# Moving where the tiles start in SBUF in a two-layer transformer kernel

## The chip, the cores and the metric

The kernel runs on one core of one Trainium2 chip. The metric is the device time of one execution in microseconds (us); lower is better. Engines are named as in the profile: PE is the matrix engine (its weight loads are shown apart as PEld), DVE the vector engine, ACT the scalar engine, POOL the general-purpose engine, and SP the engine that issues most of the DMAs. SBUF is the on-chip memory of 128 partitions. A tile takes the same bytes in each of its partitions, so its place is one number: the byte at which it starts in a partition.

## The reference

Two transformer layers are applied to one sequence of 512 positions and 1024 features, with 256 further positions of memory. The first layer is

```python
x = x + 0.5 * swiglu_ffn(rmsnorm(x, ffn1_norm_g), ffn1_w_in, ffn1_w_out)
h = rmsnorm(x, mix_norm_g)                      # q, kv, gates, conv, q_mem, merge gates = h @ w_in
x = x + (g_nsa * o_nsa + g_conv * o_conv + g_mem * o_mem) @ w_out
x = x + 0.5 * swiglu_ffn(rmsnorm(x, ffn2_norm_g), ffn2_w_in, ffn2_w_out)
```

where `o_nsa` is causal attention of 16 heads in three parts (compressed, selected and windowed keys), `o_conv` a gated convolution of width 3, and `o_mem` attention to the memory. The second layer is

```python
x = x + _mixer_block(_rms(x, norm_mix_w), ...)  # windowed attention with sinks + gated linear attention
x = x + _memory_xattn(_rms(x, norm_mem_q_w), _rms(mem, norm_mem_kv_w), ...)
x = x + _swiglu(_rms(x, norm_ffn_w), w_ffn_gate, w_ffn_up, w_ffn_down)
return _rms(x, norm_final_w)
```

All of it is given and returned in float32.

## The kernel before

**Arithmetic.** Activations are kept transposed, with features on partitions and the 512 positions along the row. Each matrix product is made of three matmuls of operands that are split in two: `three` sends high times high, high times low and low times high into one PSUM bank. So each 128x128 piece of weight costs three weight loads and three matmuls of 512 columns.

**Weights.** A unit is one DMA of up to 128x1024 floats from HBM into one of four tiles `raw`. ACT copies it into one of three tiles `whi`, rounded (`split` of `act_program`, line 1372), and DVE writes the remainder into `wlo`, which has the same place as `raw` (`split` of `dve_program`, line 1734). `dense` then makes 24 matmuls of it: for each k from 0 to 7 the stationary operand is the slice of 512 bytes at 512k of the unit, and the moving operand is a row of 2048 bytes of the activations, `XH[:, k, :]` or `XL[:, k, :]`.

**Order of the work.** The function `order` writes one list of work items, and each engine's program runs through this list. Five programs are issued, tied by semaphores. Nothing in them looks at the place of a tile.

**Places.** `sb` allocates a tile behind the last one. `place` sets a tile at a fixed column of one large block, the arena, whose first byte is `base`; the stages of the kernel use the arena in turn. In it are `RX` (the products of the two halves of each FFN, read by 1584 matmuls of the three FFNs), `MG`, `OA`, `OG` and `OM` (the operands of the output projections), `PM`, `PS`, `PW`, `P2` and `PCT` (attention weights), keys, queries, values, the tiles `pp` and `pw` of the softmax, the bias tables `TB`, the memory (`FX`, `ME`), the convolution's `CB`, and at its end the four tiles `raw`/`wlo`. Behind it stand `whi`, `XT`, `XH`, `XL`, `RB`, `cst` (constants, the identity among them), five temporary tiles `tmp`, and small tiles.

Ahead of the arena stand `vec` (176 columns of gains, biases and taps, used as per-partition scalars), `relx`, `negs` and `bg2`. A statement checks that `base` is a multiple of 1024.

**Small tiles.** `sn` is four scratch tiles for the inverse square roots; `rsqrt` uses their rows 0 to 4 (line 1762), and `rsq_out` (line 2410) gives the row of the result, row 5 of 6.

Of the kernel before, what the change touches and what calls it, by code (L numbers as in the profile page):

```python
# [14 lines left out]
P = 128  # L15
# [5 lines left out]
KF = HF // P  # L21
BIG = 1e30
EPS = 1e-6
ARENA = 28928
C_ID, C_INV, C_SEL, C_C1024, C_C256, C_ANY, C_END = 0, 128, 256, 258, 259, 260, 261


# [50 lines left out]
NVEC = _n  # L78
# [636 lines left out]
def build(nc, A, out):  # L715
# [4 lines left out]
    def sb(name, shape, dt=F32):  # L720
        return stack.enter_context(nc.sbuf_tensor("t_" + name, shape, dt))[:]

    vec = sb("vec", [P, NVEC])
    relx = sb("relx", [33, 16])
    negs = sb("negs", [P, 16])
    bg2 = sb("bg2", [P, 16])
    base = (nc.sbuf_base + 31) // 32 * 32
    assert base % 1024 == 0
    sb("arena", [P, ARENA + NRAW * UNIT])

    def place(name, at, cols, dt=F32):

        assert at + cols <= ARENA + NRAW * UNIT
        return nc.alloc_sbuf_tensor_at("t_" + name, [P, cols], dt, offset=base + 4 * at)[:]
# [3 lines left out]

    raw = [place(f"raw{i}", ARENA + i * UNIT, UNIT) for i in range(NRAW)]
    wlo = [place(f"wlo{i}", ARENA + i * UNIT, UNIT, F32R) for i in range(NRAW)]  # L740
    whi = [sb(f"whi{i}", [P, UNIT], F32R) for i in range(NHI)]
# [2 lines left out]
    XL = sb("XL", [P, KD, S], F32R)  # L744
    RB = sb("RB", [P, S])
    cst = sb("cst", [P, C_END])
    T = [sb(f"tmp{i}", [P, S]) for i in range(5)]
    FX = place("FX", 0, 5632)
    RX = place("RX", 6656, 22016, F32R)
# [25 lines left out]
    CB = [place(f"CB{q}", 19328 + q * S, S) for q in range(2)]  # L775
    CBS = [T[2:4]] * EARLY + [CB] * (KD - EARLY)
    QS = [place(f"QS{q}", (26624, 20480)[q], 2048, F32R).rearrange("p (h n) -> p h n", h=4) for q in range(2)]
# [14 lines left out]
    PW = place("PW", 12800, 4096, F32R)  # L792
    KFT = [place(f"KF{q}", 16896 + 512 * q, 512) for q in range(2)] + [T[4]]
    VW = place("VW", 17920, 2560, F32R)
# [11 lines left out]
    P2 = place("P2", 8704, 4096, F32R)  # L806
    OM = [place(f"OM{q}", 12800 + q * 1024, 1024, F32R).rearrange("p (k n) -> p k n", k=2) for q in range(2)]
    sa = [sb(f"sa{i}", [P, 8]) for i in range(RING)]
    sn = [sb(f"sn{i}", [P, 6, 16]) for i in range(4)]
    rn = sb("rn", [P, 9 * 8])  # L810
    gn = sb("gn", [P, 4, 48])
    gqn = sb("gqn", [P, 6])
    vcn = sb("vcn", [P, 64])
    vch = sb("vch", [P, 64], F32R)
    csm = sb("csm", [P, 4, 4, 4])
    KC = [sb(f"kc{q}", [P, P], F32R) for q in range(2)]
    banks = Banks([stack.enter_context(nc.psum_tensor(f"bank{i}", [P, 512], F32))[:] for i in range(8)])
    xs = nc.dram_tensor("x_kept", [D, S], F32, kind="Internal").ap()
# [75 lines left out]
    def squares(what, h, q):  # L894
        if what == "k":
            return T[h][:, 256 * q:256 * q + 256]
        return T[q] if h else T[2 + q]

# [8 lines left out]
    def pe_program(e):  # L907
# [3 lines left out]
        def mm(o, l, r, start, stop):  # L911
            return e.matmul(o, l, r, start=start, stop=stop, skip_group_check=True)  # L912
# [61 lines left out]
        def stat(item, parts, nt, g, sel, role="s"):  # L974
            b = take(role, item)
            n = len(parts) * g
            o = b[:, 0:nt * n].rearrange("p (i h) -> p i h", i=nt)
            for q, ap in enumerate(parts):
                for i in range(nt):
                    f = mm(o[:, i, q * g:(q + 1) * g], ap[:, i * P:(i + 1) * P], sel, True, True)  # L980
            f.then_inc(*full.tick(item))

        def nstat(ni):
            on.wait_ge(*calc.at(("nacc", ni, 7)))
            on.wait_ge(*d_c.at(0))
            stat(("nstat", ni), [T[4]], 4, 1, cst[:, C_C1024:C_C1024 + 1])

# [40 lines left out]
        def widefin(what, h):  # L1028
            on.wait_ge(*calc.at(("rs", "w", what, h)))
            nt = 2 if what == "k" else 4  # L1030
            spread(("widefin", what, h), rsq_out(("w", what, h), nt, 1), nt, 0, 1)
# [150 lines left out]
        def gnt():  # L1182
            b = take("d", ("gn",))
            on.wait_ge(*curve.at(("ng",)))
            for i in range(4):
                f = e.transpose(b[:, i * P:(i + 1) * P], T[4][:, i * P:(i + 1) * P], ident)
            f.then_inc(*full.tick(("gn",)))
# [8 lines left out]
        def sqfin(g, q):  # L1196
            on.wait_ge(*calc.at(("rs", "sq", g)))
            spread(("sqfin", g, q), rsq_out(("sq", g), 4, 4), 4, 2 * q, 2 * q + 2)
# [8 lines left out]
        def skfin(half, a):  # L1207
            on.wait_ge(*calc.at(("rs", "sk", half)))
            spread(("skfin", half, a), rsq_out(("sk", half), 4, 4), 4, 2 * a, 2 * a + 2)
# [4 lines left out]
        def cscore(g):  # L1214
# [3 lines left out]
            for i in range(4):  # L1218
                n = 8 * i + 8
                for r in range(4):  # L1220
                    o = b[:, i * P + r * 32:i * P + r * 32 + n]
                    l = QS[g % 2][:, r, i * P:(i + 1) * P]
                    mm(o, l, KC[0][:, g * 32:g * 32 + n], True, False)
                    f = mm(o, l, KC[1][:, g * 32:g * 32 + n], False, True)
            f.then_inc(*full.tick(("cscore", g)))
# [142 lines left out]
    def act_program(e):  # L1368
        on = Once(e)

        def copy(o, i, **how):
            return e.activation(o, i, ACT.Copy, **how)  # L1372
# [146 lines left out]
        def kc2():  # L1519
            on.wait_ge(*calc.at(("kc", 4)))  # L1520
            copy(KC[0], KX).then_inc(*x_hi.tick(("kc",)))

# [204 lines left out]
    def dve_program(e):  # L1727
# [9 lines left out]
        def low(o, x, hi, item, *more):  # L1737
            on.wait_ge(*x_hi.at(item))
            e.tensor_tensor(o, x, f32(hi), ALU.subtract).then_inc(*x_lo.tick(item, *more))  # L1739
# [267 lines left out]
        def kc2():  # L2007
# [7 lines left out]
            on.wait_ge(*calc.at(("kc", 4)))  # L2015
            low(KC[1], KX, KC[0], ("kc",))

# [384 lines left out]
    slot = {}  # L2402
# [4 lines left out]
            slot[key] = len(slot) % 4  # L2407

    def rsq_out(R, nt, n):
        return sn[slot[R]][:, 5, 0:nt * n].rearrange("p (i h) -> p i h", i=nt)  # L2410

    signals = [full, w_hi, w_lo, x_hi, x_lo, evac, copied, curve, calc, scaled, zeroed, cleared, *d_raw, *d_x, *d_m, *d_s, *d_b, *d_o,
               d_c, d_vec, d_rel, d_oh, d_w2, d_g, *d_tb, d_mask, d_gc, d_lrw]
# [91 lines left out]
```

## Time and profile before

| | us |
|---|---|
| median of three executions | 2558.79 |
| lowest, highest | 2556.7, 2560.76 |
| profiled execution | 2556.7 |
| its span, first to last instruction | 2554.9 |

The profiled execution is the fastest of the three; 1.8 us of it lie outside its span. Busy time says for how long an engine had an instruction at work; the chain of waits says which work the end waited for. Matmuls overlap each other in the profile: one of 512 columns is shown with some 390 ns though the next starts some 227 ns later. So the distance from start to start, in the timeline, is what a matmul costs in a full stretch, and its shown duration also counts the time in which it lies behind the one before it.

### The profile page before, as it was taken

To read this page: it belongs to the slowest core of one execution; us is meant where nothing else is said; L and a number is where in the kernel's file an instruction comes from. 1 tells how busy PE (TensorE), PEld (TensorE's weight loads), DVE (VectorE), ACT (ScalarE), POOL (GpSimd) and SP (SyncE) were. 2 spreads that over 40 slices of the span, in tenths; PEclk is the share of its full clock that TensorE was granted. 3 is DMA by queue.
4 is the path that set the end of the run, shared out by engine and by line. 5 is a ranking of instruction groups with operands and counts; after the bars stand their busy time and mean duration, and the time that the engine had idled before them with its cause. 6 is when DMAs were issued, how large, how long until landed. Compare 5 with 4: busy or idle time off the path is not lost.

```text
span 2554.9 us, 31373 instructions
## 1 busy us (share of the span) xinstructions
PE 2460.6 (96%) x12046; PEld 2055.1 (80%) x12046; DVE 1412.0 (55%) x2965; ACT 962.9 (38%) x1784; POOL 173.1 (7%) x236
## 2 busy tenths in 40 slices
PE   7999999999999999989999999999998997999997
PEld 6888888888887878778888888878876886788886
DVE  5435555676567566765443446666543566543444
ACT  4323334432344444553322334655422345322321
POOL 0000000100001111220000000222100002000000
PEclk9999999999999999999999999999998999899998
DMA  3454433333321111103223224211121341223222
GB/s 131 119 123 128 111 110 137 102 105 112 103 75 62 50 58 67 46 28 113 99 88 102 99 88 138 68 51 58 56 77 66 116 140 50 79 88 106 99 85 89
DMA packets 86093, 231.36 MB, mean 91 GB/s; under 512 B 8456, under 2 KB 23432, under 8 KB 85946
## 3 DMA queue, kind: packets, MB, share of 16 engines
q1 hardware_dynamic: 78480, 217.18, 26.1%
q10 hardware_dynamic: 7466, 12.19, 2.4%
q8 instruction: 97, 1.59, 0.3%
q14 instruction: 50, 0.41, 0.1%
HBM read 217.79 MB, written 11.53 MB: 90 GB/s over the span
## 4 chain that ended last, share of the span: by engine, by line
PE 87%; DVE 7%; ACT 3%; issue 2%; POOL 1%; ACTq 0%; DMA 0%; SPq 0%; DVEq 0%
PE bank L912 86%; PE bank L1082 1%; DVE t_pp L1943 1%; DVE t_PS L1739 1%; POOL t_pw L2327 1%; ACT t_pp L1492 1%; DVE t_wlo L1734 1%; ACT t_PS L1372 0%; ACT t_whi L1372 0%; DVE t_tmp L1783 0%; DVE t_QS L2036 0%; DMA t_raw<-in_f_in 0%; ACT t_XH L1372 0%; PE bank L1253 0%; ACT t_tmp L1372 0%
## 5 line engine op out<-in xcount | busy, mean ns | idle before, releaser
L912 PE MATMUL bank<-t_XH,t_whi 128*128 128x512 f32 x2064 | 819.0, 397 | 22.9 <-DVE t_XL L1743 19.6
L912 PE MATMUL bank<-t_XL,t_whi 128*128 128x512 f32 x2064 | 808.8, 392 | 0.0
L912 PE MATMUL bank<-t_XH,t_wlo 128*128 128x512 f32 x2064 | 808.6, 392 | 0.0
L1734 DVE TENSOR_TENSOR t_wlo<-t_raw,t_whi 128x1024 fp32r<-128x1024 f32 (+2 forms) x420 | 481.7, 1148 | 417.0 <-ACT t_whi L1372 413.9
L1372 ACT ACTIVATE t_whi<-t_raw 128x1024 fp32r<-128x1024 f32 (+2 forms) x420 | 415.5, 991 | 453.3 <-PE bank L912 406.5
L912 PEld LDWEIGHTS bank<-t_XH,t_whi 128*128 128x128 f32 x2064 | 391.0, 189 | 107.7 <-issue 15.0
L912 PEld LDWEIGHTS bank<-t_XH,t_wlo 128*128 128x128 f32 x2064 | 390.7, 189 | 83.5
L912 PEld LDWEIGHTS bank<-t_XL,t_whi 128*128 128x128 f32 x2064 | 391.2, 190 | 78.1
L912 PE MATMUL bank<-t_RX,t_whi 128*128 128x512 f32 x1056 | 325.0, 389 | 0.0
L1813 DVE TENSOR_TENSOR t_tmp<-bank,t_RB 128x512 f32<-128x512 f32 x178 | 122.5, 688 | 233.6 <-PE bank L912 231.3
L912 PEld LDWEIGHTS bank<-t_RX,t_whi 128*128 128x128 f32 x1056 | 198.2, 188 | 41.2
L912 PE MATMUL bank<-t_RX,t_wlo 128*128 128x512 f32 x528 | 205.4, 389 | 0.0
L2327 POOL TENSOR_SCALAR t_pw<-t_pw,t_sa 128x256 f32<-128x256 f32 (+1 forms) x80 | 71.5, 901 | 944.0 <-DVE t_sa L1956 943.5
L1372 ACT ACTIVATE t_RX<-t_tmp 128x512 fp32r<-128x512 f32 x66 | 41.7, 632 | 216.9 <-DVE t_tmp L1821 216.9
L912 PEld LDWEIGHTS bank<-t_RX,t_wlo 128*128 128x128 f32 x528 | 99.1, 188 | 20.6
L1492 ACT ACTIVATE t_pp<-t_pp,t_sa 128x256 f32<-128x256 f32 (+3 forms) x144 | 79.9, 555 | 80.7 <-DVE t_sa L1943 79.1
L2325 POOL TENSOR_SCALAR t_pp<-t_pp,t_sa,t_gn 128x128 f32<-128x128 f32 (+3 forms) x128 | 80.3, 628 | 441.2 <-DVE t_sa L1956 441.1
L1422 ACT ACTIVATE t_tmp<-t_tmp 128x512 f32<-128x512 f32 x66 | 41.7, 632 | 138.6 <-DVE t_tmp L1813 138.6
L912 PE MATMUL bank<-t_OA,t_whi 128*128 128x512 f32 x256 | 83.0, 407 | 10.7 <-DVE t_XT L1863 8.8
L1372 ACT ACTIVATE t_XH<-t_XT,t_vec 128x512 fp32r<-128x512 f32 x48 | 34.6, 721 | 118.2 <-DVE t_XT L2135 53.0
L1828 DVE SCALAR_TENSOR_TENSOR t_XT<-bank,t_XT 128x512 f32<-128x512 f32 x48 | 33.2, 692 | 80.2 <-PE bank L912 80.2
L912 PE MATMUL bank<-t_KS,t_QS 128*128 128x128 f32 (+3 forms) x256 | 69.6, 367 | 5.3 <-DVE t_sa L1943 3.5
(305 smaller groups left out, 2752.4 us busy)
## 6 DMA issues: line engine op xcount, KB each, us to landing
t_raw<-in_f_in SPq DMA_DIRECT2D x88, 512.0 KB, 3.2
t_raw<-in_f_out SPq DMA_DIRECT2D x32, 384.0 KB, 3.1
t_raw<-in_w_conv SPq DMA_DIRECT2D x24, 512.0 KB, 3.2
t_raw<-in_w_merge SPq DMA_DIRECT2D x24, 512.0 KB, 3.2
t_raw<-in_fg SPq DMA_DIRECT2D x22, 512.0 KB, 3.2
t_raw<-in_fu SPq DMA_DIRECT2D x22, 512.0 KB, 3.2
t_raw<-in_f_out SPq DMA_DIRECT2D x32, 320.0 KB, 2.8
t_raw<-in_w_g SPq DMA_DIRECT2D x16, 512.0 KB, 3.2
```

The costliest lines, as they stand in the source:

```text
L912: return e.matmul(o, l, r, start=start, stop=stop, skip_group_check=True)
L1082: f = e.transpose(b[:, j * P:(j + 1) * P], spare(hd, t)[:, j * P:(j + 1) * P], ident)
L1372: return e.activation(o, i, ACT.Copy, **how)
L1422: e.activation(s, a, ACT.Silu).then_inc(*curve.tick(("silu", f, h, m)))
L1492: e.activation(p, p, ACT.Exp, scale=-1.0, bias=s[:, 0:1], accum_out=s[:, 1:2]).then_inc(*curve.tick(("ex", t)))
L1734: e.tensor_tensor(wlo[n % NRAW][:, 0:width], raw[n % NRAW][:, 0:width], f32(whi[n % NHI][:, 0:width]), ALU.subtract).then_inc(*w_lo.tick(n))
L1739: e.tensor_tensor(o, x, f32(hi), ALU.subtract).then_inc(*x_lo.tick(item, *more))
L1813: e.tensor_tensor(o, banks[item], RB, ALU.mult).then_inc(*evac.tick(done, ("free", item)))
L1828: e.scalar_tensor_tensor(XT[:, m, :], banks[item], HALF[f], XT[:, m, :], ALU.mult, ALU.add).then_inc(*evac.tick(("free", item), *done))
L1943: e.tensor_tensor_reduce(out=spare(hd, t)[:, 0:wd], in0=banks[("score", t)][:, 0:wd], in1=score_bias(hd, i), scale=1.0, scalar=start, op0= ...
L2325: e.tensor_scalar(p, p, r, gn[:, i, k:k + 1], ALU.mult, ALU.mult).then_inc(*scaled.tick(t))
L2327: e.tensor_scalar(p, p, r, None, ALU.mult).then_inc(*scaled.tick(t))
```

## The change

The tiles `vec`, `relx`, `negs` and `bg2` are no longer allocated ahead of the arena but behind it, `vec` behind `cst` and the three others behind `csm`. The check on `base` goes. The arena is shortened by 32 columns (128 bytes), all of them between the last tile placed in it and `raw`. `sn` gets 8 rows where it had 6, and the result of the inverse square root is kept in row 7 where it was row 5.

```diff
@@ -21,7 +21,7 @@
-ARENA = 28928
+ARENA = 28896
@@ -720,12 +720,7 @@
-    vec = sb("vec", [P, NVEC])
-    relx = sb("relx", [33, 16])
-    negs = sb("negs", [P, 16])
-    bg2 = sb("bg2", [P, 16])
     base = (nc.sbuf_base + 31) // 32 * 32
-    assert base % 1024 == 0
     sb("arena", [P, ARENA + NRAW * UNIT])
@@ -744,6 +739,7 @@
     cst = sb("cst", [P, C_END])
+    vec = sb("vec", [P, NVEC])
     T = [sb(f"tmp{i}", [P, S]) for i in range(5)]
@@ -806,13 +802,16 @@
-    sn = [sb(f"sn{i}", [P, 6, 16]) for i in range(4)]
+    sn = [sb(f"sn{i}", [P, 8, 16]) for i in range(4)]
     csm = sb("csm", [P, 4, 4, 4])
+    relx = sb("relx", [33, 16])
+    negs = sb("negs", [P, 16])
+    bg2 = sb("bg2", [P, 16])
@@ -2407,7 +2406,7 @@
     def rsq_out(R, nt, n):
-        return sn[slot[R]][:, 5, 0:nt * n].rearrange("p (i h) -> p i h", i=nt)
+        return sn[slot[R]][:, 7, 0:nt * n].rearrange("p (i h) -> p i h", i=nt)
```

The instructions of each engine are the same in both kernels, with the same tiles by name and number, the same sizes and the same order: 9840 of PE (a weight load and its matmul counted as one), 2831 of DVE, 1509 of ACT, 240 of POOL and 447 of SP, from the first to the last. What differs is where the tiles start. The starts in bytes, from the two programs:

| tile | start before | its remainder by 1024 | start after | its remainder by 1024 |
|---|---|---|---|---|
| arena, `pp0`, `FX`, `ME`, `mask` | 17408 | 0 | 16512 | 128 |
| `RX` | 44032 | 0 | 43136 | 128 |
| `OA`, high and low | 99328, 115712 | 0 | 98432, 114816 | 128 |
| `PS`, high and low (first of two pairs) | 58368, 65024 | 0, 512 | 57472, 64128 | 128, 640 |
| `PCT`, `VC`, `CB`, `CH` | 86528 (first) | 512 | 85632 | 640 |
| `GA`, `GQ`, `KDt`, `VN`, `ST`, `lrw` | 29248 (`GA`) | 576 | 28352 | 704 |
| `raw0`/`wlo0` | 133120 | 0 | 132096 | 0 |
| `whi0` | 149504 | 0 | 148480 | 0 |
| `XT`, `XH`, `XL` | 161792, 178176, 194560 | 0 | 160768, 177152, 193536 | 0 |
| `RB`, `cst` | 210944, 212992 | 0 | 209920, 211968 | 0 |
| `tmp0` | 214048 | 32 | 213728 | 736 |
| `vec` | 16512 | 128 | 213024 | 32 |
| `bg2` | 17344 | 960 | 228192 | 864 |
| `sa0`, `sn0`, `rn` | 224288, 224480, 226016 | 32, 224, 736 | 223968, 224160, 226208 | 736, 928, 928 |

So the arena's tiles move by 896 bytes, the tiles from `raw` to `cst` by 1024 bytes, and the temporary tiles by 320 bytes. By 2048 the remainder of `whi`, `XT`, `XH`, `XL` and `cst` is 0 before and 1024 after.

## Rows read from the trace of the kernel before

**Rows 1.** The page: busy time by engine, and the 40 slices.
```profile
PE 2460.6 (96%) x12046; PEld 2055.1 (80%) x12046; DVE 1412.0 (55%) x2965; ACT 962.9 (38%) x1784; POOL 173.1 (7%) x236
PE   7999999999999999989999999999998997999997
PEclk9999999999999999999999999999998999899998
```
**Rows 2.** The page: shares of the chain of waits that ended last.
```profile
PE 87%; DVE 7%; ACT 3%; issue 2%; POOL 1%; ACTq 0%; DMA 0%; SPq 0%; DVEq 0%
```
**Rows 3.** PE in groups by tile: moving, stationary; busy us, mean ns; idle before.
```profile
L912 PE MATMUL bank<-t_XL,t_whi 128*128 128x512 f32 x2064 | 808.8, 392 | 0.0
L912 PE MATMUL bank<-t_RX,t_whi 128*128 128x512 f32 x1056 | 325.0, 389 | 0.0
...
L912 PE MATMUL bank<-t_PS,t_VS 128*128 128x512 f32 x96 | 30.0, 422 | 0.7 <-ACT t_PS L1372 0.7
...
L912 PE MATMUL bank<-t_PCT,t_VC 128*128 128x512 f32 x24 | 7.3, 410 | 0.0
...
L912 PE MATMUL bank<-t_P,t_VM 128*128 128x512 f32 x24 | 6.5, 406 | 1.0 <-DVE t_P L1739 1.0
```
**Rows 4.** Timeline of PE inside the first FFN: start us, length us.
```profile
240.25 0.39 PE L912 MATMUL bank<-t_XH,t_whi 128*128 128x512 f32 x1
240.48 0.39 PE L912 MATMUL bank<-t_XL,t_whi 128*128 128x512 f32 x1
240.71 0.39 PE L912 MATMUL bank<-t_XH,t_wlo 128*128 128x512 f32 x1
```
**Rows 5.** Timeline of PE from 817.3 to 817.7 us: attention weights times values.
```profile
817.23 0.84 PE L912 MATMUL bank<-t_PS,t_VS 128*128 128x512 f32 x3
```
**Rows 6.** Timeline of PE around 648.4 us: matmuls of 256 columns.
```profile
648.19 0.28 PE L912 MATMUL bank<-t_whi,t_XL 128*128 128x256 f32 x1
648.31 0.28 PE L912 MATMUL bank<-t_whi,t_XH 128*128 128x256 f32 x1
```
**Rows 7.** DVE and ACT in groups by tile, 512 columns each.
```profile
L1739 DVE TENSOR_TENSOR t_RX<-t_tmp,t_RX 128x512 fp32r<-128x512 f32 x66 | 45.7, 692 | 46.0 <-ACT t_RX L1372 46.0
L1821 DVE TENSOR_TENSOR t_tmp<-t_tmp 128x512 f32<-128x512 f32 x66 | 45.6, 692 | 2.2
...
L1492 ACT ACTIVATE t_pp<-t_pp,t_sa 128x512 f32<-128x512 f32 x32 | 23.1, 723 | 11.2 <-DVE t_sa L1943 10.0
...
L1474 ACT ACTIVATE t_tmp<-t_tmp,t_bg 128x512 f32<-128x512 f32 x16 | 11.6, 723 | 79.2 <-DVE t_tmp L1813 79.2
...
L2233 DVE TENSOR_TENSOR t_ST<-t_ST,t_KDt 128x512 f32<-128x512 f32 x4 | 2.7, 680 | 0.0
```
**Rows 8.** Line 1848, the convolution's taps on DVE: shortest, median, longest ns.
```profile
L1848 DVE SCALAR_TENSOR_TENSOR t_CB<-t_CB,t_vec,t_CB x12: 742/751/965, 679.3 to 977.5; 128x511 f32<-128x511 f32 x6, 128x510 f32<-128x510 f32 x6
L1848 DVE SCALAR_TENSOR_TENSOR t_tmp<-t_tmp,t_vec x4: 743/751/751, 548.0 to 628.9; 128x511 f32<-128x511 f32 x2, 128x510 f32<-128x510 f32 x2
```
**Rows 9.** The groups of line 1848 from 670 to 760, and from 805 to 980 us.
```profile
L1848 DVE SCALAR_TENSOR_TENSOR t_CB<-t_CB,t_vec,t_CB 128x511 f32<-128x511 f32 x3 | 2.2, 748 | 0.1
...
L1848 DVE SCALAR_TENSOR_TENSOR t_CB<-t_CB,t_vec,t_CB 128x511 f32<-128x511 f32 x3 | 2.6, 871 | 0.0
```
**Rows 10.** The tile of bias tables: who waited for it (us, times), its DMAs' landing.
```profile
  PEld bank L912: 2.1, 2
  PE bank L912: 1.5, 1
...
DMA to landing us min/median/max: 2.5/3.5/4.0
```
**Rows 11.** PE by stretch: length, busy, granted clock, DMA share, GB/s.
```profile
370.00:1140.00 770.00, 745.43 (x4120) 0.97 0.24 80
1140.00:1560.00 420.00, 417.80 (x1859) 1.00 0.32 104
2178.00:2555.00 377.00, 363.49 (x1595) 0.97 0.29 92
```

## The prediction, made before the changed kernel was run

> **What bounds the kernel now.** I read the page's busy lines first. PE is busy for 2460.6 of 2554.9 us, 96%, and its digits are 9 nearly throughout, while DVE has 55% and ACT 38% [rows 1]. The chain of waits says the same of the end: 87% PE, 7% DVE, 3% ACT, 1% POOL, and 0% for DMA [rows 2]. So a cost per matmul counts in full, and a cost on DVE or ACT counts for about a tenth.
>
> Then the groups by tile tell what PE's time is made of [rows 3]. Their shown lengths (389 to 422 ns) overlap, so the price of a matmul is read from the starts in the timeline: 240.25, 240.48, 240.71, that is 227 ns each over many of them [rows 4]. At PE's higher clock, 2.4 GHz, 512 columns are 213.3 ns; some 13.3 ns are on top. Last, the stretches show where the clock is lower: 1.00 in the dense stretch from 1140 us, 0.97 in the attention stretch before it and in the last FFN [rows 11]. The 0.97 is a mixture of 2.4 GHz and pieces at 1.2 GHz after PE had idled.
>
> **The change, part by part.** The lists of instructions are equal, engine by engine. No wait, no queue entry and no operation is added, removed or moved. Only starts differ, so everything hangs on one question: does the time of an instruction depend on where in SBUF its operands start? I take the kinds of access in turn.
>
> *PE's moving rows.* `XH` and `XL` keep their remainder by 1024 and change that by 2048, from 0 to 1024. That case is already in the trace: `RX` starts at 44032, which is 1024 by 2048, and its mean is 389 ns against 392 for `XL`, which has 0 [rows 3]. Cost 0 for these.
>
> The arena's rows come to start 128 bytes past a multiple of 1024. These are 96 matmuls on `PS`, 24 on `PCT`, 24 on the second layer's `P` [rows 3], and by the code 1584 on `RX` (1056 of them in the row), 4 projections x 8 units x 24 = 768 on `OA`, `OG` and `MG`, and 48 each on `OM` and `PM`: 2592 of 512 columns. No row shows a start at 128. The nearest is 512. In the three matmuls at 817.23 us the middle one reads the low half of `PS`, which starts at a remainder of 512, between two that read the high half at 0. The three together take 0.84 us [rows 5], which is 2 x 0.227 + 0.389: no slower and no faster than rows at 0. I take 0 for this. The ends of the range: the lower one is that the whole 13.3 ns came from rows that start together, -13.3 x 2592 = -34.5 us; the upper one is the widest gap between groups of these rows, `PS` (a third of whose moving rows start at 512) 422 against `P` 406, 16 ns x 2592 = +41 us. Both ends are far from the row at 817.23, which is the like case, so the value sits by that row. The 422 is a mean that also counts groups which begin from rest; the warm triple of the same tile has none of it.
>
> *PE's stationary slices.* In each unit they start at 512k, so a remainder of 0 and of 512 alternate against a moving row that always starts at 0, and the distance from start to start is the same for all [rows 4]. After the change the moving row's place against them shifts by 128 for the arena's rows. Matmuls of 256 columns start 0.12 us apart [rows 6], where 256 columns are 106.7 ns: the same 13.3 ns on top at half the row. What is on top is therefore a fixed price per matmul, not a share of the row, and this speaks against both ends above. Cost 0.
>
> *DVE and ACT.* Their operands are an unplanned test, since the tiles of one form start at different remainders. DVE's subtraction takes 692 ns with `RX` (0) and 692 ns on `tmp` alone (32); the sum on `ST` and `KDt` (576) takes 680 [rows 7]. ACT with a per-partition scalar takes 723 ns both with `pp` and `sa` and with `tmp` and `bg2` [rows 7]; `bg2` stands at a multiple of 64, and of the six `sa` every other one 32 past such a multiple, the very step that `vec`, `negs` and `bg2` make. Cost 0. The bounds: the 12 ns between 692 and 680 are 1.8%, and 10% of the span is DVE's and ACT's share of the chain [rows 2], 255 us x 1.8% = 4.6 us, either way.
>
> One row seems to contradict this. Line 1848 has a longest time of 965 ns on `CB`, which starts at 512, and 751 on `tmp`, at 32 [rows 8]. But its shortest and its median on `CB` are 742 and 751, as on `tmp`, with the same start in all twelve. A start can't lengthen some of them only. The three of 511 columns from 670 to 760 us take 748 ns in the mean, the three from 805 to 980 us 871 [rows 9]; by the code POOL scales the attention weights of the first layer's heads in the second of these stretches. Behind this row stands a rule of the Trainium skill, "SBUF — State Buffer", section on the engine side's shared port: a DVE instruction with two SBUF inputs and a POOL instruction that reads SBUF hold each other up. By that rule the place of a tile has no part in it and the change adds 0; read as the price of a start it would be 214 ns on each of some hundreds of DVE instructions. The trace agrees with the rule, since the four on `tmp`, outside POOL's stretch, are all short.
>
> *POOL.* Its tiles `pp` and `pw` all start at a remainder of 0 before, so no row shows another start. It is 1% of the chain, 25 us [rows 2]. I take 0, as for the other engines; by DVE's 1.8% it would be 0.5 us either way.
>
> *DMA.* By the code every weight goes to `raw`, whose remainder stays 0, and DMA has 0% of the chain [rows 2]. The bias tables, the memory and the masks now land 128 bytes past. A table load lands after 3.5 us in the median and 4.0 at most, and all that PE ever waited on `TB` is 2.1 us in two waits of its weight loads and 1.5 in one of its matmuls [rows 10]. If each of the three waits grew by the whole 0.5 us between the median and the longest, it would be 1.5 us; the lower end is -3.6 us, all of these waits. I take 0, since 13 of 16 loads had nobody waiting.
>
> *Row 7 for row 5 of `sn`, and 8 rows for 6.* The same operations on other bytes of a scratch tile: 0. The removed check costs nothing on the chip.
>
> **Sum.** 0 + 0 + 0 + 0 + 0 on the profiled execution's own 2556.7 us (span 2554.9 and 1.8 outside). That one is the fastest of the three; the median lies 2.1 above. Forecast 2558.8 us for the median. The spread of the executions shown, 2556.7 to 2560.76, is the same program, so I expect nothing finer.
>
> **Rivals.**
>
> *Rows that straddle cost more (slower).* A row of 2048 bytes that starts at a multiple of 1024 covers two such pieces; started at 128 it touches three. If PE pays at the third, each of the 2592 matmuls is longer, in stretches where PE never waits, so all of it shows. The price from rows: `PCT`, at 512, has a mean of 410 ns, and `P`, at 0, 406 [rows 3], both in groups that begin from rest: 4 ns x 2592 = 10.4 us, 2569.2 us. It decides from 2 ns a matmul (5.2 us). For it: every dense operand before starts at 0, so the trace is silent on 128. Against: the low half of `PS` at 512 also touches three, at no price [rows 5], and `PCT` comes in groups of three where `P` comes in six, so fewer of its matmuls are warm, which alone makes its mean higher.
>
> *Equal starts are what costs (faster).* Before, `RX`, `XH`, `whi`, `wlo` and `XT` all start at multiples of 1024, so PE, ACT and DVE may step through the same part of the memory together; staggered by 128 the arena's rows would be free of it. If it gave the whole 13.3 ns back: 2558.8 - 34.5 = 2524.3 us; at a quarter of that, 2550.2. Against: the same 13.3 ns at 256 columns, and with weight slices at 0 and at 512 alike [rows 4, 6].
>
> *A DMA that starts off a boundary is slower.* By the trace this is the 1.5 us above, 2560.3 us, inside what can't be told from no change. The Trainium skill, "DMA: Bandwidth & Descriptors", section on how a descriptor splits into AXI transactions, says that one which doesn't start at a multiple of 256 bytes begins at the boundary below and carries bytes for nothing; by that rule the tables, at 128 past such a multiple, would take one transaction more each row and `raw` none, and the time would be the one just given. No row here shows a DMA of the same size at both kinds of start.
>
> *The clock falls otherwise.* PE's lower clock follows its idle time, and in the attention stretch 0.97 over 770 us is 46 us at 1.2 GHz, which cost at most 23 us of PE's time [rows 11]. Were a tenth of such pieces to fall elsewhere, 2 to 3 us either way. This is part of the forecast's spread.
>
> **How the numbers follow.** No change, 0.70, of which 0.03 falls out of the band by the spread of executions (0.02 faster, 0.01 slower). Straddling rows, 0.17, all slower. Equal starts, 0.10, all faster. A slower DMA, 0.03, of which 0.02 with something exposed that these rows don't show. A measurement of this kernel can tell 0.2%, 5.1 us, from no change. Faster by more than that: 0.12; within: 0.68; slower: 0.20. For 8 in 10 the range takes the forecast's spread of some 4 us and the straddling case whole, and of the other rival the quarter: 2550 to 2570 us.
>
> **What would show it.** Right: every group of matmuls keeps its mean within 1 ns, `RX` 389 and `XL` 392; the starts stay 227 ns apart in the FFN stretches; the stretch from 1140 to 1560 us still holds 1859 matmuls; the DVE subtraction on `RX` stays at 692. The straddling rival shows as a second distance in the second half of each FFN, on `RX` alone, with `XH` and `XL` unchanged. The equal-starts rival shows as a distance below 227 there. The DMA case shows in who waits for `TB`. I am wrong in the main step if any form of instruction has another length with its tile's new start. The weakest point is that no start at 128 is in the trace.

## The result, and the profile after

The changed kernel takes 2575.65 us (median of four, 2573.95 to 2577.6) where the kernel before took 2559.17 beside it: a ratio of 1.0065, 95% interval 1.0048 to 1.0083. It is slower by 16.5 us. The forecast of no change was wrong, and the time lies above the range.

The page after has the same shape. The span grew from 2554.9 to 2572.0 us and PE's busy time by 19.9 us, while those of the other engines moved by at most 1.9 us [rows 1]:

```profile
PE 2480.5 (96%) x12046; PEld 2057.0 (80%) x12046; DVE 1412.8 (55%) x2965; ACT 962.9 (37%) x1784; POOL 171.2 (7%) x236
...
PEclk9999999999999999999999999999998999899998
...
PE 87%; DVE 7%; ACT 3%; issue 2%; POOL 1%; DMA 0%; ACTq 0%; SPq 0%; DVEq 0%
```

The lines of the code stand one lower after the change (911 for 912). PE's groups by tile (moving, stationary), as in [rows 3], with four more that matter:

```profile
L911 PE MATMUL bank<-t_XL,t_whi 128*128 128x512 f32 x2064 | 809.7, 392 | 0.0
L911 PE MATMUL bank<-t_RX,t_whi 128*128 128x512 f32 x1056 | 331.6, 395 | 0.0
L911 PE MATMUL bank<-t_RX,t_wlo 128*128 128x512 f32 x528 | 208.6, 395 | 0.0
...
L911 PE MATMUL bank<-t_MG,t_whi 128*128 128x512 f32 x128 | 41.3, 405 | 2.2 <-DVE t_MG L1742 2.2
L911 PE MATMUL bank<-t_OG,t_whi 128*128 128x512 f32 x128 | 40.3, 396 | 0.0
L911 PE MATMUL bank<-t_PS,t_VS 128*128 128x512 f32 x96 | 30.1, 422 | 0.7 <-ACT t_PS L1371 0.7
...
L911 PE MATMUL bank<-t_PM,t_MV 128*128 128x512 f32 x48 | 11.6, 390 | 0.0
L911 PE MATMUL bank<-t_PCT,t_VC 128*128 128x512 f32 x24 | 7.3, 411 | 0.0
L911 PE MATMUL bank<-t_P,t_VM 128*128 128x512 f32 x24 | 6.5, 407 | 1.0 <-DVE t_P L1738 1.0
```

`XL` keeps 392 ns. `RX` went from 389 to 395, `OG` from 391 to 396. But `PS`, `PM`, `PCT` and `P` moved by the same 896 bytes and kept their means within 1 ns. This suggests that a start at 128 costs nothing by itself: those four are multiplied with stationary tiles of the arena, which moved along, while `RX`, `MG`, `OA` and `OG` are multiplied with `whi` and `wlo`, whose remainders stayed.

One more group points the same way. For the memory's values the roles are turned round: the moving rows are in `whi` and `wlo`, still at a multiple of 1024, and the stationary slices are in the tile `MX` of the arena, now 128 past one. These 96 matmuls are longer too, though their rows kept their remainder. The 32 with `wlo`, before and then after (the 64 with `whi` went from 398 to 401 ns):

```profile
L912 PE MATMUL bank<-t_wlo,t_MX 128*128 128x512 f32 x32 | 12.5, 390 | 0.0
```

```profile
L911 PE MATMUL bank<-t_wlo,t_MX 128*128 128x512 f32 x32 | 12.6, 394 | 0.0
```

The timeline of PE in the first FFN's products on `RX`, where the kernel before has 227 ns from start to start (start us, length us):

```profile
148.97 0.63 PE L911 MATMUL bank<-t_RX,t_whi 128*128 128x512 f32 x2
149.43 0.39 PE L911 MATMUL bank<-t_RX,t_wlo 128*128 128x512 f32 x1
149.66 0.63 PE L911 MATMUL bank<-t_RX,t_whi 128*128 128x512 f32 x2
150.13 0.40 PE L911 MATMUL bank<-t_RX,t_wlo 128*128 128x512 f32 x1
150.37 0.63 PE L911 MATMUL bank<-t_RX,t_whi 128*128 128x512 f32 x2
```

From 148.97 to 150.37 are six matmuls, 233.3 ns each. Single distances on `RX` are mostly 229 and 237. Two stretches of the first FFN, of the kernel before and then of the changed one, show that only the one that is mostly on `RX` (126 to 196 us) lost matmuls, and the one on `XH` and `XL` (196 to 318 us) none:

```profile
126.00:196.00 70.00, 70.00 (x310) 1.00 0.51 120
196.00:318.00 122.00, 122.00 (x541) 1.00 0.45 121
```

```profile
126.00:196.00 70.00, 70.00 (x303) 1.00 0.50 118
196.00:318.00 122.00, 122.00 (x541) 1.00 0.46 120
```

DVE and ACT are as they were [rows 7]:

```profile
L1738 DVE TENSOR_TENSOR t_RX<-t_tmp,t_RX 128x512 fp32r<-128x512 f32 x66 | 45.7, 693 | 46.1 <-ACT t_RX L1371 46.1
L1820 DVE TENSOR_TENSOR t_tmp<-t_tmp 128x512 f32<-128x512 f32 x66 | 45.7, 692 | 2.2
L2232 DVE TENSOR_TENSOR t_ST<-t_ST,t_KDt 128x512 f32<-128x512 f32 x4 | 2.7, 680 | 0.0
```

```profile
L1491 ACT ACTIVATE t_pp<-t_pp,t_sa 128x512 f32<-128x512 f32 x32 | 23.1, 723 | 10.6 <-DVE t_sa L1942 9.3
L1473 ACT ACTIVATE t_tmp<-t_tmp,t_bg 128x512 f32<-128x512 f32 x16 | 11.6, 723 | 79.9 <-DVE t_tmp L1812 79.9
```

**The account.** 1584 matmuls on `RX`, 768 of the projections and 48 on `OM` are multiplied with weights from `whi` and `wlo`: 2400. At the 233.3 - 226.7 = 6.6 ns of `RX` for each this would be 10.5 + 5.1 + 0.3 = 15.9 us. The start-to-start distances of the trace say a little less: those on `OA`, `MG`, `OG` and `OM` went from 227.2 to 232.6 ns in the mean (the few over 260 ns, at gaps and at the lower clock, left out), so their 816 come to 4.4 us, and the 96 on `MX` to 0.3. Together 15.2 of the 16.5 us, whose interval of 12.3 to 21.2 us holds either sum.

`MG` shows 405 rather than 395 ns because a piece of lower clock fell into that projection of this execution. The run below with the arena at 256, which doesn't have the price, has such a piece there too (400 ns), so it isn't part of the price. The stretch of `MG` before, and then after:

```profile
1146.30:1190.10 43.80, 43.72 (x193) 1.00 0.39 133
```

```profile
1147.70:1194.10 46.40, 45.94 (x191) 0.96 0.38 125
```

### The profile page after: what moved, and what is told of

Its sections match the earlier page's. It is cut to its first block, busy times and chain, and to the rows that moved or that the text cites. A ratio compares the mean times of both kernels' runs of the same rounds, so it can differ in the third digit from the quotient of the medians.

```text
span 2572.0 us, 31373 instructions
## 1 busy us (share of the span) xinstructions
PE 2480.5 (96%) x12046; PEld 2057.0 (80%) x12046; DVE 1412.8 (55%) x2965; ACT 962.9 (37%) x1784; POOL 171.2 (7%) x236
## 4 chain that ended last, share of the span: by engine, by line
PE 87%; DVE 7%; ACT 3%; issue 2%; POOL 1%; DMA 0%; ACTq 0%; SPq 0%; DVEq 0%
PE bank L911 86%; PE bank L1081 1%; DVE t_pp L1942 1%; DVE t_PS L1738 1%; DVE t_wlo L1733 1%; POOL t_pw L2326 1%; ACT t_pp L1491 1%; ACT t_PS L1371 0%; ACT t_whi L1371 0%; DVE t_tmp L1782 0%; DVE t_QS L2035 0%; DMA t_raw<-in_f_in 0%; ACT t_XH L1371 0%; DVE t_tmp L2095 0%; PE bank L1252 0%
## 5 line engine op out<-in xcount | busy, mean ns | idle before, releaser
L911 PEld LDWEIGHTS bank<-t_XH,t_whi 128*128 128x128 f32 x2064 | 391.6, 190 | 108.4 <-issue 15.2
L911 PE MATMUL bank<-t_RX,t_whi 128*128 128x512 f32 x1056 | 331.6, 395 | 0.0
```

## The experiments

**Theories.** M: a moving row that starts off a multiple of 1024 costs (the straddling rival of the prediction). R: a matmul costs more when its moving row and the stationary slices start at different remainders. E: the price comes from ACT or DVE beside PE. Another possible cause was `vec`, `tmp` or `sn`.

### Everything shifted together

```diff
 (against the changed kernel)
-ARENA = 28896
+ARENA = 28928
-    sn = [sb(f"sn{i}", [P, 8, 16]) for i in range(4)]
+    sn = [sb(f"sn{i}", [P, 6, 16]) for i in range(4)]
-        return sn[slot[R]][:, 7, ...
+        return sn[slot[R]][:, 5, ...
```

> The changed kernel with the weights, X, RB and cst also shifted, so that the arena and everything behind it start at a remainder of 128 (ARENA 28928; sn back to 6 rows and row 5, to make room). vec stays behind cst, tmp now at 864. Theory R: the moving rows and the weights agree again; the 16.5 us are gone, 2559 us, RX back to 389 ns, XL at 392. Theory M: XH and XL are hit too, 6192 + 2592 matmuls x 6.6 ns = 58 us, 2617 us, XL near 398 ns. If instead the moves of vec, tmp or sn were the cause: unchanged, 2575 us.

Measured: 2558.88 us against 2560.01, ratio 0.9996 (0.9987 to 1.0005). Its groups:

```profile
L911 PE MATMUL bank<-t_XL,t_whi 128*128 128x512 f32 x2064 | 808.4, 392 | 0.0
L911 PE MATMUL bank<-t_RX,t_whi 128*128 128x512 f32 x1056 | 325.3, 389 | 0.0
```

All dense operands start at 128, and nothing is lost. M is refuted. `vec` stands behind `cst` here as in the changed kernel (128 bytes further on), and `tmp` at a third place (864), so those moves cost nothing that this can tell, either. `sn` was put back in this run, but the next shows that the whole loss comes without it.

### Only what stands behind the arena shifted

```diff
 (against the kernel before)
-ARENA = 28928
+ARENA = 28960
```

> The kernel before with everything from raw on shifted by 128 (ARENA 28960): arena at 0, weights and X at 128; vec, relx, negs and bg2 where they were before. Theory R: as in the changed kernel the arena's rows and the weights disagree, 2400 matmuls x 6.6 ns = 16 us, 2575 us, RX at 395 ns, XL at 392. Theory M: RX at 389 and XL at 398 ns, 6192 x 6.6 = 41 us, 2600 us.

Measured: 2578.19 us, ratio 1.0068 (1.0048 to 1.0087): the loss of the changed kernel, with `vec`, `relx`, `negs` and `bg2` in place, `sn` with its 6 rows, and `RX` at a multiple of 1024.

```profile
L912 PE MATMUL bank<-t_XL,t_whi 128*128 128x512 f32 x2064 | 809.0, 392 | 0.0
L912 PE MATMUL bank<-t_RX,t_whi 128*128 128x512 f32 x1056 | 331.7, 395 | 0.0
```

### Only the weights shifted

Two small tiles fill the gap behind `whi`, so that `XT`, `XH`, `XL`, `RB`, `cst` and `tmp` stay at their remainders.

```diff
 (against the kernel before)
-ARENA = 28928
+ARENA = 28960
+    KC = [sb("kc0", [P, P], F32R)]
+    sn = [sb("sn0", [P, 6, 16])]
     XT = sb("XT", [P, KD, S])
```

> The kernel before with raw, wlo and whi alone shifted by 128 (kc0 and sn0 fill the gap behind whi, so that XT, XH, XL, RB and cst stay at 0), arena at 0. Theory R: every product with a weight unit disagrees, 6192 on XH and XL + 2400 on the arena's rows = 8592 x 6.6 ns = 57 us, 2616 us, with XL and RX both some 6 ns longer. Theory M: no moving row has another remainder, 2559 us.

Measured: 2600.58 us, ratio 1.0167 (1.0144 to 1.0191), so +40.6 us. R's direction and tiles are right, both groups are hit:

```profile
L914 PE MATMUL bank<-t_XL,t_whi 128*128 128x512 f32 x2064 | 819.9, 397 | 0.0
L914 PE MATMUL bank<-t_RX,t_whi 128*128 128x512 f32 x1056 | 331.3, 395 | 0.0
```

The size is under the expected 57 us. A part is the price with this sign: 232.5 ns a matmul, 5.8 over 226.7, which is 50 us for 8592. Where the rest went can be read by finding the same matmuls in both traces. The dense stretch from 1140 to 1560 us of the kernel before [rows 11] holds 1859 matmuls, and the same 1859 take 430.2 us here: 10.2 us more, which is 5.6 ns for each of the 1819 that disagree. The attention stretch ahead of it, before and then here:

```profile
850.00:1140.00 290.00, 273.90 (x1550) 0.94 0.14 46
```

```profile
866.70:1154.60 287.90, 272.19 (x1550) 0.95 0.14 47
```

Its 472 disagreeing matmuls added nothing; the stretch is even 2.1 us shorter, with less of it at the lower clock. Here PE also waits for other engines (it is busy for 273.9 of 290 us), so a longer matmul can disappear in a wait. This is one execution of each kernel, so it fits the 9 to 16 us that are missing, and doesn't prove where all of them went.

### PE alone, first sweep

The kernel loads x, rounds it, and PE runs series of 56 matmuls; ACT and DVE stand still.

```diff
+                for k in range(7):
+                    c = k * P + s // 4
+                    f = e.matmul(banks[n % 8], W[:, c:c + P], M[:, k * 512 + m // 4:k * 512 + m // 4 + 512], ...)
```

> This kernel computes nothing of the reference: it loads x, rounds it, and PE alone runs 29 series of 56 matmuls of 512 columns, each with its weight load; only the remainders by 1024 at which the moving row and the stationary slice start differ from series to series. The distance from start to start tells the price. Theory R (a matmul is longer when the moving row and the stationary slice start at different remainders by some block size): 227 ns for (0,0), (64,64), (128,128), (256,256) and for 512 against 0; about 233 ns for 128 against 0 and for 0 against 128. Theory M (only the moving row's own start counts): 233 ns for (128,128) and all moving starts that aren't 0 or 512, and 227 ns for moving 0 against stationary 64 to 384. Theory E (the price comes from ACT or DVE working beside PE): 227 ns in every series, since they stand still here.

Mean distance from start to start in ns, from the last 53 matmuls of each series; the stationary slices at 0:

| row starts at | ns | row starts at | ns |
|---|---|---|---|
| 0, 768 | 226.67 | 256, 512 | 226.9 |
| 32 | 233.33 | 288 | 233.33 |
| 64 | 228.83 | 320 | 228.83 |
| 96 | 233.58 | 352 | 233.58 |
| 128, 640, 896 | 233.3 | 384 | 233.33 |
| 160 | 234.31 | 416 | 234.31 |
| 192 | 233.33 | 448 | 233.35 |
| 224 | 233.35 | 480 | 233.35 |

Rows at 0 with slices at 64: 233.33; at 128: 232.35; at 256: 227.06; at 384: 232.25. Both shifted alike: (64, 64) and (128, 128) 227.29, (256, 256) 226.67, and (384, 128) 226.65. The agreeing pairs that show 226.9 to 227.3 differ from 226.67 only at the start of the series: up to ten distances of 224 to 236 ns, and then 226.67 to the end in all of them. The groups of five stretches show the same in the shown length; they are rows at 0, 64, 128, 256, and rows and slices both at 128:

```profile
L65 PE MATMUL bank<-t_mov,t_sta 128*128 128x512 f32 x41 | 9.5, 389 | 0.0
...
L65 PE MATMUL bank<-t_mov,t_sta 128*128 128x512 f32 x36 | 8.4, 391 | 0.0
...
L65 PE MATMUL bank<-t_mov,t_sta 128*128 128x512 f32 x40 | 9.5, 395 | 0.0
...
L65 PE MATMUL bank<-t_mov,t_sta 128*128 128x512 f32 x41 | 9.5, 389 | 0.0
...
L65 PE MATMUL bank<-t_mov,t_sta 128*128 128x512 f32 x42 | 9.7, 389 | 0.0
```

R holds and E is refuted: the price is there with PE alone. It has a period of 256 bytes, in the difference between row and slice, not in either start. That is why no group of the kernel before showed it: its slices alternate between 0 and 512, its `PS` rows start at 0 and 512, all multiples of 256. With the roles turned the price is not quite the same (232.35 for a slice at 128, 233.3 for a row at 128).

### The changed kernel with its arena at 256, and at 320

```diff
 (against the changed kernel; for 320: ARENA 28848, a pad of 48, base += 192)
-ARENA = 28896
+ARENA = 28864
+    sb("pad", [P, 32])
+    base += 128
     sb("arena", [P, ARENA + NRAW * UNIT])
```

> The changed kernel with the arena 128 bytes further on, so that it starts at a remainder of 256 by 1024, and raw, whi and all behind them where the changed kernel has them (ARENA 28864, a pad of 32 columns). vec, tmp and sn as in the changed kernel. Theory R with the period of 256 bytes that the first sweep shows: rows and slices agree, 2559 us as before, RX 389 ns. If a remainder by 512 or 1024 were what counts: 2575 us and RX 395.

> The same with the arena at a remainder of 320, 64 past a multiple of 256 (ARENA 28848, a pad of 48 columns). The first sweep has 228.83 ns at 64 and at 320, 2.2 ns over an agreeing pair: 2400 x 2.2 = 5.2 us, 2564 us, ratio 1.002. If any disagreement cost the same as 128 does: 2575 us.

Measured: 2560.6 us at 256, ratio 1.0005 (0.9996 to 1.0014), and 2566.79 us at 320, ratio 1.003 (1.0018 to 1.0041), which is 7.7 us with 4.6 to 10.5, around the 5.2 expected. `RX` at 256, then at 320:

```profile
L913 PE MATMUL bank<-t_RX,t_whi 128*128 128x512 f32 x1056 | 325.0, 389 | 0.0
```

```profile
L913 PE MATMUL bank<-t_RX,t_whi 128*128 128x512 f32 x1056 | 327.3, 391 | 0.0
```

The first keeps every other part of the change: `vec` behind `cst`, the small tiles behind `csm`, 8 rows of `sn` with the result in row 7. A pad of 128 bytes, taken out of the arena's slack, gives all of the loss back. The run at 320 has more than the steady 2.2 ns in two places. The 48 matmuls on `PM` and `MV` have row and slice both 64 past a multiple of 256, so they agree. Still each of their four groups of 12 goes 228, 229, 233 or 234, 236, 224, 231, 235 or 236 and so on before it comes to 227: within 1 ns the sequence with which the series (64, 64) of the sweep begins. The first group, in the kernel before and then here:

```profile
530.40 2.88 PE L912 MATMUL bank<-t_PM,t_MV 128*128 128x512 f32 x12
```

```profile
532.15 2.92 PE L913 MATMUL bank<-t_PM,t_MV 128*128 128x512 f32 x12
```

So going from pairs at 0 (`XH` and `whi`) to pairs at 64 costs some 40 ns once, though both agree in themselves. In the changed kernel, going to the same tiles at 128 costs 4 ns once (231 and then 227). And the last projection on `OA` (from 2080 us) has 233.3 ns from start to start, where `RX`, with the same starts modulo 1024, has 228.8. A part of it, beside the 391 of `RX` above:

```profile
L913 PE MATMUL bank<-t_OA,t_whi 128*128 128x512 f32 x86 | 27.1, 397 | 0.0
```

The changed kernel has two steady prices as well, 233.3 ns on `RX` and some 232.4 on `MG` and the last `OA`. So the starts decide whether a series pays, but don't fix how much. What else decides it was not tested.

None of these versions is faster than the kernel before, and the sweeps have no difference that gives under 226.6 ns for 512 columns.

### PE alone, second and third sweep

```diff
+            for i in range(56):
+                k = i % 7
+                m, s = ms[i % len(ms)] // 4, k * P + ss[i % len(ss)] // 4
```

> PE alone again, 27 series of 56 matmuls, nothing of the reference computed. First question, which weight load collides with a row: its own, which ends before the row starts, or the next one, which runs while the row is read. With the moving rows at 0 and the stationary slices in turn at 0, 0, 128: if the next load counts, the distance is longer (some 233 ns) behind the second matmul of each three, whose row runs beside the load at 128, and 227 behind the two others; if its own load counts, it is longer behind the third. With rows (0, 0, 128) and slices in the same turn (0, 0, 128) own pairs agree and next pairs disagree twice in three; with slices (0, 128, 0)... the other way round. Second question, the period: the first sweep gave 227 at multiples of 256, 229 at 64 and 320, 233 elsewhere; I expect 16, 48, 80, 240 and 4 to cost 6 to 7 ns like 32, and 272 the same as 16. Third, shorter rows: 256 columns should cost half of it, 3 ns, if the price grows with the row, and 6.7 if it is per matmul; 64 and 128 columns are bounded by the weight load and shouldn't move.

The period holds: rows at 16 and at 272 both have 231.67 ns. The other starts: 4 235.13, 48 233.33, 80 231.10, 240 233.33; rows and slices both at 32, 226.67. Not every difference costs the 6 to 7 ns I expected. The sign matters only through the difference: a row at 0 with the slice at 192 has 228.88, as a row 64 past its slice, and with the slice at 32, 233.33, as a row at 224. The price hangs on the row's length: 384 columns 173.75 (agreeing) and 175.94 (row at 128), 256 columns 119.94 and 118.62, 128 columns 111.65 and 111.65. So it is neither per matmul nor in proportion. The agreeing ones have some 13.3 ns on top of their columns at each length (119.94 over 106.7, 173.75 over 160), as the prediction read from the rows of 256. The series of 64 columns and the last one ran in part at the lower clock and are left out here.

On which load collides, one slice in three at 128 made two of three distances long, 232.4 and 234.4, where either theory had one. One row in three at 128 made one of three long (228.8 in the mean). The third sweep asked that alone:

```diff
+PAIRS = [(512, Z, Z), (512, Z, at(2)), (512, at(2), Z), (512, at(2), at(1)), (512, at(2), at(2)), ...
```

> PE alone, 14 series of 126 matmuls of 512 columns in a pattern of six; nothing of the reference computed. Rows and slices start at 0 except at the named places of the six, where they start at 128. The second sweep left open which load a row collides with: one slice in three at 128 cost 13.3 ns per three, one row in three 6.6. Per six, over the 1360 ns of the series with all at 0: theory N (a row pays 6.7 ns if the next load disagrees with it) gives 6.7 for one slice off, 6.7 for one row off, 0 for row 2 with slice 3 off, 13.3 for row 2 with slice 1, 2 or 4 off. Theory O (its own load) gives 0 for row 2 with slice 2 off and 13.3 for the others. Theory B (a row pays once if either its own or the next load disagrees) gives 13.3 for one slice off, 6.7 for one row off, 6.7 for row 2 with slices 2 and 3 off, 20 for rows at 0 with slices 2 and 3 off. If none of them fits, the price isn't a sum over single pairs.

Over the 1360.0 ns of six that agree, measured over the last 120 distances of each series: one slice off 13.3, one row off 6.7; row 2 with slice 1, 2, 3 or 4 off 20.0, 26.7, 23.3, 20.0; row 2 with slices 2 and 3 off 29.0; slices 2 and 3 off, rows at 0, 35.0; slices 2, 3 and 4 off 30.7; rows 2 and 3 off 20.0. B has the first two right and fails on row 2 with slices 2 and 3 (6.7 expected); N and O fail at once. So the price is not a sum over single pairs, and how the two streams meet inside PE or SBUF stays open. Going from one start to another within a series costs as much as a steady disagreement: two slices in six at 128 cost 35.0 ns, and all six 6 x 5.7 = 34 by the first sweep.

## Why the prediction was wrong

- **The step that failed** is "PE's moving rows ... I take 0", together with "PE's stationary slices ... Cost 0". The prediction took a start as a property of one operand and looked for its price at the nearest other start, 512. The runs show a price on the difference between row and slice, modulo 256. Against that period, 0 and 512 are the same start, so "the like case" at 817.23 us [rows 5] compared equal with equal. The same holds for the slices "at 0 and at 512 alike". The prediction even named what counts ("the moving row's place against them shifts by 128") and put it at 0 by the argument from 256 columns. The weakness was named (no start at 128 in the trace), but 0.70 on it was far too much.
- **The argument from 256 columns** [rows 6], that a fixed 13.3 ns on top excludes a price that grows with the row, was sound for the equal-starts rival, which indeed didn't happen, and no argument on what a disagreement adds: that comes on top of the 13.3, and the second sweep shows that it does change with the row's length.
- **The straddling rival** came nearest, 2569.2 us against 2575.65. It had the place right (the arena's rows, each FFN's second half, `XH` unchanged) and both its price (4 ns for 5.4 to 6.6) and its mechanism wrong: with all starts at 128 nothing is lost. It also charged `PS`, `PM`, `PCT` and `P`, which pay nothing.
- **DVE, ACT** at 0: right, 692 to 693 and 680 and 723 ns, as in [rows 7]. The reading of the long taps on `CB` [rows 8, 9] as another engine's doing was not contradicted, and not tested.
- **POOL and DMA** at 0: right in that both keep their share of the chain, 1% and 0%. The waits for `TB` went from 3.6 to 4.2 us in all, within the 1.5 us of the prediction's bound.
- **`sn`'s rows and `vec`'s place** at 0: right as far as 0.1% can tell, by the run with the arena at 256.
- **What would show it:** the list named a second distance on `RX` alone with `XH` and `XL` unchanged, and that is what the trace has.

## What to carry to other kernels

Give the moving rows and the stationary slices of a long matmul starts that differ by a multiple of 256 bytes. Whether both are at 0 or both at 128 made no difference that this kernel could show; but keep all pairs that follow one another at the same remainder, since going from pairs at 0 to pairs at 64 was not free. When small tiles are moved or a block is resized, look at what that does to the remainder of everything behind it, and pad. And when a trace is to tell what a start costs, first ask modulo what its starts differ: examples that are all alike in the unknown block size say nothing.

## What the runs showed of the hardware

- With 512 columns of this float32 form and a weight load for each, PE starts a matmul every 226.67 ns at 2.4 GHz if row and slice agree modulo 256 bytes, and every 228.8 to 235.1 ns if they don't. PE alone shows it, so it needs no other engine. A row 64 past its slice was the cheapest of the starts tried in the series (228.8), but in one projection of the full kernel it had 233.3.
- After a change of starts the first distances differ, even where the new pair agrees: up to ten of them, from 224 to 236 ns, before 226.67 in the sweep, and the same in the kernel with its arena at 320.
- With 256 columns the disagreement gave 118.6 in place of 119.9 ns, and with 128 columns no difference.
- The instructions of DVE and ACT shown above kept their time to 1 ns when `RX` went from 0 to 128, `tmp` from 32 to 736, `ST` and `KDt` from 576 to 704, and `bg2` from 960 to 864 by 1024. No group of instructions of these two engines changed its median by more than 6 ns.
